# Gates of one token block by a zeroed DRAM matrix and adding indirect transfers, in an encoder block with a product-key expert layer

## What is computed

```python
def peer_ffn(x, w_query, sub_keys, expert_u, expert_v):
    ...
        q = (xb @ w_query).reshape(TB, PH, 2, PEER_QUERY_DIM // 2)
        s = jnp.einsum('thpd,hpkd->thpk', q, sub_keys).astype(jnp.float32)
        v_half, i_half = lax.top_k(s, K)
        cand = v_half[:, :, 0, :, None] + v_half[:, :, 1, None, :]
        cidx = i_half[:, :, 0, :, None] * PEER_N_KEYS + i_half[:, :, 1, None, :]
        top_s, pos = lax.top_k(cand.reshape(TB, PH, K * K), K)
        idx = jnp.take_along_axis(cidx.reshape(TB, PH, K * K), pos, axis=-1)
        g = jax.nn.softmax(top_s, axis=-1).astype(xb.dtype)
        u = expert_u[idx]
        a = jax.nn.gelu(jnp.einsum('td,thkd->thk', xb, u), approximate=False)
        return jnp.einsum('thk,thkd->td', g * a, expert_v[idx])
```

## Time and profile before

| | us |
|---|---|
| median of 3 runs | 1009.66 (1009.54 to 1009.88) |
| the profiled execution, its own time | 1009.48 |
| its span in the trace | 1007.7 |
| PE busy | 998.6 (99% of the span) |
| DVE busy | 836.5 (83%) |
| ACT busy | 612.8 (61%) |
| POOL busy | 81.0 (8%) |

### The profile page before, as it was taken

The page is one execution under the profiler, slowest core; times in us unless marked ns, Lnnn a source line. Parts: engine busy times, 40 slices in busy tenths (PEclk is TensorE's granted clock), DMA queues, the critical chain, the costliest instruction groups (busy, mean ns, idle before and its releaser), DMA issues.

```text
span 1007.7 us, 20517 instructions
## 1 busy us (share of the span) xinstructions
PE 998.6 (99%) x6937; PEld 916.0 (91%) x6937; DVE 836.5 (83%) x1668; ACT 612.8 (61%) x1167; POOL 81.0 (8%) x38
## 2 busy tenths in 40 slices
PE   9999999999999999999999999999999999999997
PEld 9889899999999999999999999978888888888886
DVE  7988868769998899999999999777777777777776
ACT  6456754656545478888888888544444444444444
POOL 0000000377850000000000000000000000000000
PEclk9999999999999999999999999999999999999999
DMA  8744345645677776667666666897777777777771
GB/s 310 236 136 143 120 153 182 231 151 206 204 223 240 231 219 206 206 208 208 208 209 208 207 207 211 285 305 235 234 235 234 234 234 232 235 234 235 234 234 69
DMA packets 87893, 214.93 MB, mean 213 GB/s; under 512 B 9744, under 2 KB 43280, under 8 KB 87440
## 3 DMA queue, kind: packets, MB, share of 16 engines
q1 hardware_dynamic: 87248, 213.07, 65.7%
q10 hardware_dynamic: 576, 0.93, 0.3%
HBM read 195.08 MB, written 18.87 MB: 212 GB/s over the span
## 4 chain that ended last, share of the span: by engine, by line
PE 96%; DVE 2%; DMA 0%; issue 0%; ACT 0%; ACTq 0%; DVEq 0%
PE pO L1172 35%; PE pO L1455 18%; PE pTT L1487 17%; PE pM L1487 17%; PE pSS L1429 2%; PE pTT L1429 2%; PE pSS L1237 1%; DVE wlos L719 1%; PE pSS L1393 1%; DMA xcol<-in_xcol 0%; PE pM L1276 0%; PE pTT L1256 0%; PE pTT L1498 0%; PE pM L1270 0%; PE pTT L1249 0%
## 5 line engine op out<-in xcount | busy, mean ns | idle before, releaser
L480 ACT ACTIVATE whis<-raw 128x1024 fp32r<-128x1024 f32 x326 | 344.5, 1057 | 203.4 <-PE pM L1487 170.9
L1080 DVE TENSOR_TENSOR wlos<-raw,whis 128x1024 fp32r<-128x1024 f32 x125 | 153.3, 1226 | 87.7 <-ACT whis L480 87.6
L719 DVE TENSOR_TENSOR wlos<-raw,whis 128x1024 fp32r<-128x1024 f32 x169 | 205.4, 1219 | 11.9 <-ACT whis L480 11.5
L1172 PE MATMUL pO<-xhi,whis 128*128 128x256 f32 x752 | 212.1, 282 | 0.0
L1172 PE MATMUL pO<-xlo,whis 128*128 128x256 f32 x752 | 210.0, 279 | 0.0
L1172 PE MATMUL pO<-xhi,wlos 128*128 128x256 f32 x752 | 209.8, 279 | 0.0
L1455 PE MATMUL pO<-xlo,whis 128*128 128x256 f32 x512 | 143.4, 280 | 0.0
L1172 PEld LDWEIGHTS pO<-xhi,whis 128*128 128x128 f32 x752 | 141.1, 188 | 2.4 <-issue 2.0
L1455 PE MATMUL pO<-xhi,wlos 128*128 128x256 f32 x512 | 143.0, 279 | 0.0
L1455 PE MATMUL pO<-xhi,whis 128*128 128x256 f32 x512 | 143.0, 279 | 0.0
L1172 PEld LDWEIGHTS pO<-xlo,whis 128*128 128x128 f32 x752 | 141.3, 188 | 0.0
(11 more groups left out here) (251 smaller groups left out, 1868.2 us busy)
## 6 DMA issues: line engine op xcount, KB each, us to landing
raw<-in_stream SPq DMA_DIRECT2D x199, 512.0 KB, 3.7
raw<-in_vrows SPq DMA_DIRECT2D x128, 512.0 KB, 3.5
a_scratch<-ast SPq DMA_DIRECT2D x128, 128.0 KB, 1.9
aring<-a_scratch SPq DMA_DIRECT2D x128, 128.0 KB, 3.2
biasm<-in_bias SPq DMA_DIRECT2D x8, 256.0 KB, 5.2
keysT<-in_keys SPq DMA_DIRECT2D x1, 1024.0 KB, 5.6
h_scratch<-h1tok SPq DMA_DIRECT2D x1, 1024.0 KB, 6.2
htok<-h_scratch SPq DMA_DIRECT2D x1, 1024.0 KB, 9.7
```

The costliest lines, as they stand in the source:

```text
L480: act.activation(whi[s], raw[s][:], ACT.Copy).then_inc(hi_ready, 1)
L719: dve.tensor_tensor(wlo[t % RING], raw[t % RING][:], whi[t % RING].bitcast(F32), ALU.subtract).then_inc(lo_ready, 1)
L1080: dve.tensor_tensor(wlo[s], raw[s][:], whi[s].bitcast(F32), ALU.subtract).then_inc(lo_ready, 1)
L1172: last = pe.matmul(dst, st, mv, start=(c == 0 and q == 0), stop=(c == len(terms) - 1 and q == 2))
```

## The change

Half of the gates, those of tokens 0 to 127, no longer come from one-hot products. POOL fills an SBUF tile with zeros, and SP writes it 32 times (256 KB each) to a new DRAM tensor `g_scratch` of 16384 x 128 floats, in step with the loads of tiles 16 to 47. When the picks of block 0 are known, DVE works out for each pick the element's address, (first digit x 128 + second digit) x 128 + token (two new instructions), and POOL issues 128 indirect transfers: each takes one pick of all 128 tokens, and adds the 128 gates to 128 elements of `g_scratch`. They go in 8 groups of 16, one group per head; ahead of each group but the first POOL waits until the earlier ones have landed.

`G` is now [128, 128 tokens, 128], and the one-hot steps are 32, three in eight U tiles, the last in U tile 122. One block is transposed instead of two. For each V tile SP loads another 64 KB, a row of `g_scratch`, into a ring `gring` of four, and DVE's multiplication is two instructions of 128 columns. The first four such loads are issued with those of `aring`, one U tile later than before, after a wait for all indirect transfers. `held` and `upad` keep the other tensors where they were.

```diff
-G_STEPS = T // GTOK
+G_STEPS = P // GTOK
...
-    if at < 0 or at % 4 == 3:
+    if at < 0 or at % 8 not in (0, 3, 6):
         return None
-    k = at // 4 * 3 + at % 4
+    k = at // 8 * 3 + at % 8 // 3
...
+            sp.wait_ge(zeros_ready, 1)
+            with sp.Fori(0, ZERO_PARTS // RAW) as g:
+                for s in range(RAW):
+                    load(g * RAW + (s + 4 * RAW), s, stream[bass.ds(g * RAW + (s + 4 * RAW), 1)])
+                    sp.dma_start(g_parts[bass.ds(g * RAW + s, 1)], zeros).then_inc(g_zeroed, 16)
...
-                if i == G_LAST:
+                if s == 1:
 
                     sp.wait_ge(g_done, 2 * G_STEPS)
+                    sp.wait_ge(g_scattered, 16 * PH * TOPK)
                     for q in range(4):
                         sp.wait_ge(a_stored[q % 2], 16 * (q // 2 + 1))
                         sp.dma_start(aring[q][:], a_dram[q]).then_inc(a_landed[q], 16)
+                        sp.dma_start(gring[q], g_tiles[q]).then_inc(a_landed[q], 16)
...
+            pool.wait_ge(g_zeroed, 16 * ZERO_PARTS)
+            pool.wait_ge(offsets_ready, 1)
+            pool.wait_ge(gates_ready, 1)
+            for h in range(PH):
+
+                if h:
+                    pool.wait_ge(g_scattered, 16 * TOPK * h)
+                for k in range(TOPK):
+                    n = h * TOPK + k
+                    pool.indirect_dma_start(g_dram, bass.IndirectOffsetOnAxis(goff[:, n:n + 1], 0), gval[:, h, k:k + 1], None,
+                                            compute_op=ALU.add).then_inc(g_scattered, 16)
...
+                if b == 0:
+                    flat = [route[:, 0, q].rearrange("p h k -> p (h k)") for q in range(2)]
+                    link(dve.tensor_scalar(gtmp[:], flat[1], float(P), K("part"), ALU.mult, ALU.add))
+                    dve.scalar_tensor_tensor(goff, flat[0], float(NK * P), gtmp[:], ALU.mult, ALU.add).then_inc(offsets_ready, 1)
...
-                dve.tensor_tensor(wfull[s % 2][:], aring[s][:], mine.rearrange("p t o -> p (t o)"), ALU.mult).then_inc(w_ready, 1)
+                dve.tensor_tensor(wfull[s % 2][:, 0:P], aring[s][:, 0:P], gring[s], ALU.mult)
+                dve.tensor_tensor(wfull[s % 2][:, P:T], aring[s][:, P:T], mine.rearrange("p t o -> p (t o)"), ALU.mult).then_inc(w_ready, 1)
...
                     pe.wait_ge(routed, 1)
-                    turn_route(0)
                     turn_route(1)
```

More of the change, by code:

```diff
@@ L91 @@
 GSUB = 2
-G_STEPS = T // GTOK
+G_STEPS = P // GTOK
 G_FIRST = 39
-G_LAST = G_FIRST + (G_STEPS - 1) // 3 * 4 + (G_STEPS - 1) % 3
+G_LAST = G_FIRST + (G_STEPS - 1) // 3 * 8 + (G_STEPS - 1) % 3 * 3
+ZERO_PARTS = 32
+ZERO_COLS = NK * NK // ZERO_PARTS
 HOTS = 3
@@ L116 @@
 _at = 0
-for _name, _n in (("ident", P), ("cos", T), ("sin", T), ("iota16", 16), ("mask", GRID_W)):
+for _name, _n in (("ident", P), ("cos", T), ("sin", T), ("iota16", 16), ("mask", GRID_W), ("part", 1)):
     CONST[_name] = (_at, _at + _n)
@@ L155, in act_takings, with build @@
     return sum(not evac_engine(x)[0] for x in range(t))
-def build(nc, stream, vrows, const, keys, bias, lamv, gfin, h1_dram, a_dram, out):
+def build(nc, stream, vrows, const, keys, bias, lamv, gfin, h1_dram, a_dram, g_dram, out):
     with ExitStack() as top:
@@ L228, in build @@
                 gsum = sbs(router, "gsum", [P, 2, TB, PH])
-        G = sbs(top, "G", [P, T, NK])
+        G = sbs(top, "G", [P, P, NK])
+        held = sbs(top, "held", [P, T - P, NK])
+        gring = [held[:, s, :] for s in range(4)]
+        goff = held[:, P - 2, :].bitcast(U32)
+        gval = held[:, P - 1, :].rearrange("p (h k) -> p h k", h=PH)
         fin = sbs(top, "fin", [P, 12])
@@ L249, in build @@
             ghi = [sbs(vphase, f"ghi{s}", [P, T], F32R) for s in range(2)] + ghi_more
+        zeros = ghot[:].rearrange("p u t h i -> p (u t h i)").bitcast(F32)[:, 0:ZERO_COLS]
+        g_parts = g_dram.rearrange("(n p f) o -> n p (f o)", p=P, f=ZERO_COLS)
+        g_tiles = g_dram.rearrange("(n p f) o -> n p (f o)", p=P, f=P)
         rows = [raw[s][:].rearrange("p c n -> p (c n)") for s in range(TB)]
@@ L340, in build @@
         low_hots_ready = sem("low_hots_ready")
+        zeros_ready = sem("zeros_ready")
+        g_zeroed = sem("g_zeroed")
+        offsets_ready = sem("offsets_ready")
+        gates_ready = sem("gates_ready")
+        g_scattered = sem("g_scattered")
         g_done = sem("g_done")
@@ L461, in _ @@
             pool.memset(ones[:], 1.0).then_inc(ones_ready, 1)
+            pool.memset(zeros, 0.0).then_inc(zeros_ready, 1)
             def low(t, s):
@@ L1518, in constants @@
     put("ident", np.eye(P, dtype=np.float32))
+    put("part", np.arange(P, dtype=np.float32)[:, None])
     put("iota16", np.arange(16, dtype=np.float32)[None, :])
```

26 lines of the change are left out of this document (15 added, 11 removed).

## The result

| | before | after |
|---|---|---|
| median, us | 1009.72 (1009.54 to 1009.88) | 1025.01 (1024.41 to 1025.41) |
| the profiled execution | 1009.48 | 1025.0 |
| its span | 1007.7 | 1023.2 |

The ratio is 1.0151, with a 95% interval of 1.0133 to 1.0169: the change makes the kernel slower by 15.3 us, where 13.5 us less were forecast.

The account below looks back on a forecast made before the run. PE, busy 998.6 of 1007.7 us, was taken to bound the kernel. 1009.48 - 15.0 (gate steps) - 0.3 (transposes) + 2.0 (passage from U to V) = 996.2 us; range 993.5 to 1012.

Parts of the forecast that it names:

- the scatter is too slow: Rival: each POOL transfer costs over 1.96 us, V loads queue behind SP's wait, PE runs dry; 1054 us at 2.41; chance 0.14.
- What is removed: On PE, 32 of 64 gate steps (15.0 us) and three of six transposes (0.3 us) go, all on the path.
- the passage: From U to V: later V tile loads behind the ring loads, stalls of 0.3 and 1.7 us, +2.0 us, bounds 0 and 4.
- The scatter's price: POOL's indirect transfers: 1.2 us each, with landings 168 us in all, ending near 523, 97 us early, so no cost.
- The limit of 1.96 us per transfer: Most that each of POOL's 128 transfers may take: 265.7 us available less 14.7 for landings.
- The start of the scatter: Ahead of U: gates known at about 354.8 instead of 353.8, covered by 0.8 us before PE's transposes, so no cost.
- The deadline: SP's wait ahead of the first ring loads, reached at about 620.5, leaving 265.7 us for the transfers.
- Zeros and V: In U, 32 zero writes of 8.4 MB cost nothing; in V, DMA share about 0.80 and DVE's products 667 ns, no cost.
- The shared port: Rival in U: DVE's L1059 one-hot instructions wait for POOL's transfers, DVE falls behind PE; 1031 us; chance 0.07.
- the forms that I had set aside: VectorE's two-input forms; the forecast took L1059 as port candidate instead, by a rule on copies and tensor-scalar forms.
- The estimate of 1142 us: Time if each of 128 GpSimd transfers took the skill's 3100 ns beside a VectorE copy: 397 us against 251 available.
- Crowding: Rival in U: 16384 scattered elements crowd the DMA engines, share 1.14, loads up to 37 us late; 998 to 1007; chance 0.08.

Follow-up runs that it names:

- half of the heads: The changed kernel with the scatter of heads 0 to 3 alone, 64 transfers instead of 128, other gates of block 0 left out: 998.39 us median, ratio 0.989.

## Why the prediction was wrong

The forecast was 996.2 us and the range ended at 1012.0; it took 1025.0. The rival "the scatter is too slow" (0.14) came true, with the mechanism as it was described: SP stands in its wait, the V tiles' loads are queued behind it, and PE runs dry.

- **What is removed: right.** The step is still 0.47 us, and with half of the heads the time was 997.3 in the profiled execution and 998.4 in the median, with 2.5 us of waits at the passage.
- **The scatter's price: this step failed.** It took 1.2 us, between ends of 0.34 and 2.41 us, on the argument that the issue row should be nearest. The real price without any neighbour is 1.54 + 0.30 = 1.84 us, 82 us more for 128. This took the margin from 97 us to 15: 128 x 1.84 = 235.5, and with the 14.7 us of landings 250.2 of the 265.7. The rest took it over: 24.5 us of holding by VectorE, 9.6 us of long gaps, and 3.7 us more in landings (18.4 without the 0.30 already counted, against 14.7). 250.2 + 24.5 + 9.6 + 3.7 = 288.0 us, measured 288.2. The limit of 1.96 us per transfer was right: with 2.09 measured, gaps and holding included, (2.09 - 1.96) x 128 = 16.6 us, 5.8 us more in landings and 1.5 for the last one make 23.9, which is SP's wait. With bounds that lay on both sides of the limit, 0.14 for this rival was too little; nothing in the trace spoke for 1.2 rather than for 2.0.
- **The start of the scatter: 354.8 forecast, 358.28 in the profiled execution**, 354.75 where the front was undisturbed (half of the heads). The deadline moved by as much (624.1 for 620.5), so it cost nothing there, but it added 3.8 us to the time.
- **The lower clock behind a pause was not in the sum** of any rival: 1.8 us at 655.
- **The passage: right in sum.** +2.0 forecast; 2.5 and 2.0 us of waits without an overrun. With half of the heads they are 1.3 us at 632 and 1.2 at 651, where 0.3 and 1.7 were forecast, so the sum hit by some luck. The first comes as described: the third V tile's high part starts late (at 629.05, after ACT waited 2.93 us for the load), and the first wait was gone where the ring loads stood behind that load (1.0 left, at 649).
- **Zeros and V: right.** PE had no wait in U; V's share is 0.80 as forecast, and L1110 and L1111 take 0.29 + 0.37 = 0.66 us (0.667 forecast).
- **The shared port: right pair, wrong victim.** Of the earlier trace rows it was said that the two instructions end together; DVE's cast ended at 292.21 + 2.80 = 295.01, 0.42 us behind POOL's subtraction. DVE's one-hot instructions (L1098) went from 344 to 355 ns, no delay to speak of. It is POOL's transfers that are held, by the forms that I had set aside. The estimate of 1142 us from the Trainium skill's 3100 ns (SBUF — State Buffer, "A bandwidth-pool intuition that's wrong (but worth ruling out)") is far too much, since only 44 of the 128 transfers were stretched at all; but the page's mechanism, blocked until the end of DVE's instruction and not slowed in proportion, is what the trace shows, with 1.41 us behind the end.
- **Crowding: not a cost.** The share rose to 0.88, not 1.14, PE stayed full in U beside all 128 transfers, and the time was no lower without any transfer (998.9) than with 64 (998.4).

## What to carry to other kernels

A new operation whose price isn't in the trace, used 128 times against a deadline, is a bet on that price: where its bounds lie on both sides of the break-even, the odds are near even, and the design should first be given the slack that makes the price not matter (here a start 44 us earlier, a reordered queue and the small sums together turned +1.5% into -1.3%). GpSimd's indirect transfers should not be put beside long chains of VectorE instructions with two SBUF inputs, and where they must be, a short sum between them let a transfer through in nine cases of nine, while splitting them made the transfers longer in both kernels where it was tried.

## What the runs showed of the hardware

- An indirect, adding transfer issued by GpSimd takes 1.28, 1.41 and 1.54 us for 16, 64 and 128 elements, and 0.30 us pass until the next.
- At a few places there is a gap of 1.8 to 4.8 us: with 128 elements ahead of transfers 61, 114 and 121 in every run that had them, with 64 elements ahead of 114 only, with 16 never. What makes it is open.
- Waiting for the landing of such a group takes 2.4 to 4.7 us with 128 elements (1.8 to 4.2 with 16); a plain load took 2.1 from issue to landing.
- A transfer that begins beside a VectorE instruction with two SBUF inputs, or a copy, of 0.4 to 2.3 us, is held until it ends. If another of the kind follows directly, it is held on in some cases (50 of 150 at one border, nearly all of those that had begun 0.24 to 0.30 us ahead of it) and gets through in the others; the longest took 10.12 us. Copies also held transfers at their end. Sums over columns did not hold one, tensor-scalar instructions by 0.14 us at most. VectorE loses next to nothing by this: L755 took 1220 ns in the mean, 1218 before.
